# Two of a weight tile's six matmuls made one of 512 columns, its halves added by VectorE

## The reference

```
layer 0:  h = rmsnorm(x); [u | v | z | xbc | dt] = h @ w_in
          x += concat(gmlp(u, v), ssd(z, conv4(xbc), dt)) @ w_out
layer 1:  h = rmsnorm(x); [q | k | v | g] = h @ w_in          # 8 heads
          x += retention(q, k, v, g) @ w_out
each:     h = rmsnorm(x)
          x += (silu(conv3(h @ w_gate)) * (h @ w_up)) @ w_down   # 2816 wide
          x += (p @ w_proj) * sigmoid(rmsnorm(x) @ w_gate_ple)
y = rmsnorm(x)
```

## Time and profile before

| | |
|---|---|
| runs | 1811.79, 1813.09, 1813.15 us (median 1813.09) |
| profiled execution | 1812.7 us, span 1810.9 us |
| granted TensorE clock | 0.996 of full, mean |
| TensorE matmul | 1793.2 us busy, 14029 matmuls |
| VectorE | 930.8 us |
| GpSimd | 834.1 us |
| ScalarE | 635.6 us |
| HBM | 88 GB/s over the span |

### The profile page before, as it was taken

How to read it: one execution, slowest core, us unless ns; L and a number is a source line. 1 busy time by engine, 2 the same in 40 slices (tenths; PEclk the granted TensorE clock), 3 DMA queues, 4 the chain that set the end, 5 groups by cost and what they waited for, 6 DMA issues and landing times.

```text
span 1810.9 us, 34242 instructions
## 1 busy us (share of the span) xinstructions
PE 1793.2 (99%) x14029; PEld 1751.2 (97%) x14029; DVE 930.8 (51%) x1514; ACT 635.6 (35%) x973; POOL 834.1 (46%) x410
## 2 busy tenths in 40 slices
PE   9999999999999999999999999999999999999997
PEld 8999889999999999999999999999899999999997
DVE  6556776666514524546544441444555425515465
ACT  6434564543222222344333331233332213212342
POOL 4323312674545544476533334333365435544663
PEclk9999999999999999999999999999999999999998
DMA  6222232222342232232222222222222222222231
GB/s 236 81 74 72 82 106 72 81 94 94 105 141 82 93 97 91 70 104 83 95 69 76 78 70 91 79 79 69 67 82 93 93 85 89 94 92 85 61 102 50
DMA packets 58389, 161.04 MB, mean 89 GB/s; under 512 B 6817, under 2 KB 19105, under 8 KB 58289
## 3 DMA queue, kind: packets, MB, share of 16 engines
q1 hardware_dynamic: 52224, 151.03, 25.6%
q10 hardware_dynamic: 6064, 8.61, 1.5%
HBM read 153.94 MB, written 5.67 MB: 88 GB/s over the span
## 4 chain that ended last, share of the span: by engine, by line
PE 94%; DVE 3%; ACT 1%; issue 1%; DMA 0%; POOL 0%; ACTq 0%; DVEq 0%; POOLq 0%
PE proj L321 84%; PE Q L1045 7%; PE proj L1045 2%; ACT arena L667 1%; DVE arena L1786 1%; DMA x<-in_x 0%; PE Q L1340 0%; DVE arena L1777 0%; DVE arena L1597 0%; PE Q L1225 0%; DVE arena L1914 0%; PE Q L1271 0%; POOL arena L660 0%; PE Q L1305 0%; DVE rstd L372 0%
## 5 line engine op out<-in xcount | busy, mean ns | idle before, releaser
L417 POOL TENSOR_TENSOR w_lo<-w_raw,w_hi 128x1024 fp32r<-128x1024 f32 (+2 forms) x276 | 663.2, 2404 | 768.0 <-ACT w_hi L343 757.9
L321 PE MATMUL proj<-op_hi,w_hi 128*128 128x256 f32 x4208 | 880.1, 290 | 1.9 <-DVE op_lo L1527 0.8
L321 PE MATMUL proj<-op_hi,w_lo 128*128 128x256 f32 x4208 | 869.3, 288 | 0.0
L321 PE MATMUL proj<-op_lo,w_hi 128*128 128x256 f32 x4208 | 862.2, 286 | 0.0
L321 PEld LDWEIGHTS proj<-op_hi,w_hi 128*128 128x128 f32 x4208 | 671.8, 188 | 17.0 <-issue 12.4
L321 PEld LDWEIGHTS proj<-op_lo,w_hi 128*128 128x128 f32 x4208 | 674.4, 188 | 0.0
L321 PEld LDWEIGHTS proj<-op_hi,w_lo 128*128 128x128 f32 x4208 | 670.4, 188 | 0.0
L343 ACT ACTIVATE w_hi<-w_raw 128x1024 fp32r<-128x1024 f32 (+2 forms) x276 | 284.6, 1031 | 657.8 <-PE proj L321 651.3
L1597 DVE TENSOR_TENSOR arena<-proj,rstd 128x512 f32<-128x512 f32 x141 | 97.5, 691 | 218.4 <-PE proj L321 208.6
L1604 DVE TENSOR_TENSOR x<-proj,x 128x512 f32<-128x512 f32 x72 | 49.7, 690 | 240.3 <-PE proj L321 240.3
L667 ACT ACTIVATE arena<-arena 128x128 f32<-128x128 f32 (+6 forms) x298 | 129.1, 475 | 59.8 <-DVE arena L1600 29.8
(11 more groups left out here) (190 smaller groups left out, 1032.8 us busy)
## 6 DMA issues: line engine op xcount, KB each, us to landing
w_raw<-in_w_gu SPq DMA_DIRECT2D x88, 512.0 KB, 3.4
w_raw<-in_w_down SPq DMA_DIRECT2D x32, 512.0 KB, 3.4
w_raw<-in_w_heads_a SPq DMA_DIRECT2D x30, 512.0 KB, 3.4
w_raw<-in_w_heads_b SPq DMA_DIRECT2D x18, 512.0 KB, 3.4
w_raw<-in_w_gate SPq DMA_DIRECT2D x16, 512.0 KB, 3.4
w_raw<-in_w_xbc SPq DMA_DIRECT2D x12, 512.0 KB, 3.4
w_raw<-in_w_down SPq DMA_DIRECT2D x16, 384.0 KB, 3.1
w_raw<-in_w_v SPq DMA_DIRECT2D x8, 512.0 KB, 8.0
```

Source lines behind the costliest of these rows:

```text
L321: last = nc.tensor.matmul(proj[:, 2 * g.mod(2) + half, 0:size], w[:, lo:lo + P], o[:, at:at + size], start=(k == 0 and j == 0), stop=(k == ...
L417: nc.gpsimd.tensor_tensor(w_lo[:, c:c + width], w_raw[:, c:c + width], w_hi[:, c:c + width], ALU.subtract).then_inc(w_lo_done, 1)
```

## The change

In `slab`, the two matmuls of the high weights over the early tokens, one with the high and one with the low operand, become one of 512 columns. Its moving operand has two runs of 256 columns (the high and low parts, which therefore now lie in one buffer, `op_both`), and its output fills bank `2q`: the first half has high by high, the second high by low. The low weights' product accumulates on the first half. The late tokens keep three matmuls of 288 columns in bank `2q + 1`, so a tile has five matmuls. VectorE adds the halves: in `scaled` and in the up product a `tensor_reduce` writes their sum to a new SBUF buffer `half_sum`, the late half is multiplied straight from PSUM, and the early half is multiplied from `half_sum`; in `add_to_x` the second half is added to x ahead of the rest, with a wait between. The groups in `PLAIN` (v and dt, pp, the last one) keep six matmuls and the old reading.

```diff
--- before.py
+++ after.py
@@ -139,6 +139,12 @@
         return p.g0 + (s - p.s0 + 1) * p.m
 
     DT_GROUP = PH["v"].g0 + KD
+    PLAIN = [*range(DT_GROUP + 1), *(PH[f"pp{layer}"].g0 + m for layer in range(2) for m in range(KD)),
+             PH["gate1"].g0 + KD - 1]
+
+    def summed_before(g):
+
+        return g.c - sum(p < g.c for p in PLAIN)
 
     ctx = ExitStack()
     with ctx:
@@ -154,10 +160,10 @@
 
 
         x = sb("x", KD * T)
-        op_hi, op_lo = [sb("op0_hi", KD * T, R)], [sb("op0_lo", KD * T, R)]
+        op_both = [sb("op0", 2 * KD * T, R)]
         early = nc.sbuf_base
-        op_hi.append(sb("op1_hi", KD * T, R))
-        op_lo.append(sb("op1_lo", KD * T, R))
+        op_both.append(sb("op1", 2 * KD * T, R))
+        op_hi, op_lo = [op[:, 0:KD * T] for op in op_both], [op[:, KD * T:2 * KD * T] for op in op_both]
         ARENA = 15200
         arena = sb("arena", ARENA)
         ssq = sb("ssq", T)
@@ -182,6 +188,7 @@
         a_row = sb("a_row", SH)
         conv_state = sb("conv_state", XBC * 3)
         conv_tail = sb("conv_tail", XBC * 6)
+        half_sum = nc.alloc_sbuf_tensor_at("half_sum", [P, HALF], F, offset=nc.sbuf_base)
         w_dt = sb("w_dt", 8 * SH)
         w_dt_hi = sb("w_dt_hi", 8 * SH, R)
         w_dt_lo = sb("w_dt_lo", 8 * SH, R)
@@ -313,14 +320,23 @@
                     if ready:
                         pe.wait_ge(ready[0], ready[1] + k)
                     lo = slot * SLAB + (k * ph.m + m) * P
-                    passes = ((w_hi, op_hi[ops]), (w_hi, op_lo[ops]), (w_lo, op_hi[ops]))
-                    for j, (w, o) in enumerate(passes):
-                        for half in range(2):
-                            size = HALF if half == 0 else HALF + TS
-                            at = (k0 + k) * T + half * HALF
-                            last = nc.tensor.matmul(proj[:, 2 * g.mod(2) + half, 0:size], w[:, lo:lo + P],
-                                                    o[:, at:at + size], start=(k == 0 and j == 0),
-                                                    stop=(k == ph.kt - 1 and j == 2))
+                    high, low = w_hi[:, lo:lo + P], w_lo[:, lo:lo + P]
+                    first, end = k == 0, k == ph.kt - 1
+                    q = 2 * g.mod(2)
+                    at = (k0 + k) * T
+                    early = slice(at, at + HALF)
+                    late = slice(at + HALF, at + T)
+                    rest = proj[:, q + 1, 0:HALF + TS]
+                    if g.c in PLAIN:
+                        nc.tensor.matmul(proj[:, q, 0:HALF], high, op_hi[ops][:, early], start=first, stop=False)
+                        nc.tensor.matmul(proj[:, q, 0:HALF], high, op_lo[ops][:, early], start=False, stop=False)
+                    else:
+                        nc.tensor.matmul(two(proj[:, q, :]), high, two(op_both[ops][:, :])[:, :, early], start=first,
+                                         stop=False)
+                    nc.tensor.matmul(rest, high, op_hi[ops][:, late], start=first, stop=False)
+                    nc.tensor.matmul(rest, high, op_lo[ops][:, late], start=False, stop=False)
+                    nc.tensor.matmul(proj[:, q, 0:HALF], low, op_hi[ops][:, early], start=False, stop=end)
+                    last = nc.tensor.matmul(rest, low, op_hi[ops][:, late], start=False, stop=end)
                 if ph.kt - 1 in ks:
                     last.then_inc(tile_done, 1)
 
@@ -1590,17 +1606,33 @@
             tt = nc.vector.tensor_tensor
             stt = nc.vector.scalar_tensor_tensor
 
-            def scaled(g, dst, signal=None, rows=P, factor=None, f_at=0):
-
-                by = rstd if factor is None else factor
+            def out_times(g, dst, by, rows=P):
+
                 dve.wait_ge(tile_done, (g + 1).v)
-                a = tt(two(dst(0, TP)), out_prompt(g, rows), two(by[0:rows, f_at:f_at + TP]), mul)
+                if g.c in PLAIN:
+                    return tt(two(dst(0, TP)), out_prompt(g, rows), two(by[0:rows, 0:TP]), mul)
+                q = 2 * g.mod(2)
+                dve.wait_ge(tile_read, g.v)
+                nc.vector.tensor_reduce(half_sum[:, :], proj[:, q, :].rearrange("p (h e) -> p e h", h=2), AX.X, add)\
+                    .then_inc(sem("halves_added"), 1)
+                tt(dst(HALF, HALF), proj[:, q + 1, 0:HALF], by[:, HALF:TP], mul)
+                dve.wait_ge(sem("halves_added"), (g + (summed_before(g) - g.c + 1)).v)
+                return tt(dst(0, HALF), half_sum[:, :], by[:, 0:HALF], mul)
+
+            def scaled(g, dst, signal=None, rows=P):
+
+                by = rstd
+                a = out_times(g, dst, by, rows)
                 if signal:
                     a.then_inc(sem(signal), 1)
-                tt(dst(TP, TS), out_sample(g, rows), by[0:rows, f_at + TP:f_at + T], mul).then_inc(tile_read, 1)
+                tt(dst(TP, TS), out_sample(g, rows), by[0:rows, TP:T], mul).then_inc(tile_read, 1)
 
             def add_to_x(g, n):
                 dve.wait_ge(tile_done, (g + 1).v)
+                if g.c not in PLAIN:
+                    xa = part(x, n, 0, HALF)
+                    tt(xa, proj[:, 2 * g.mod(2), HALF:TP], xa, add).then_inc(sem("halves_added"), 1)
+                    dve.wait_ge(sem("halves_added"), (g + (summed_before(g) - g.c + 1)).v)
                 tt(two(part(x, n, 0, TP)), out_prompt(g), two(part(x, n, 0, TP)), add)
                 tt(part(x, n, TP, TS), out_sample(g), part(x, n, TP, TS), add).then_inc(tile_read, 1)
 
@@ -1772,7 +1804,7 @@
                 at = q * (T + 6)
                 if n >= 2:
                     dve.wait_ge(sem("x_silu"), n - 1)
-                scaled(group("xbc", n), lambda c, w: xpad[:, at + 3 + c + (3 if c else 0):at + 3 + c + (3 if c else 0) + w],
+                scaled(group("xbc", n), lambda c, w: xpad[:, at + 3 + c + (3 if c >= TP else 0):at + 3 + c + (3 if c >= TP else 0) + w],
                        "x_steps")
                 nc.vector.tensor_copy(xpad[:, at + 3 + TP:at + 6 + TP], part(conv_state, n, 0, 3, 3))\
                     .then_inc(sem("x_steps"), 1)
@@ -1898,8 +1930,8 @@
                             at = q * (T + 4)
                             if t.k or t.c >= 2:
                                 dve.wait_ge(sem("f_silu"), (t + -1).v)
-                            scaled(group(gu, n), lambda c, w: gpad[:, at + 2 + c + (2 if c else 0):
-                                                                   at + 2 + c + (2 if c else 0) + w],
+                            scaled(group(gu, n), lambda c, w: gpad[:, at + 2 + c + (2 if c >= TP else 0):
+                                                                   at + 2 + c + (2 if c >= TP else 0) + w],
                                    "f_steps")
                             nc.vector.tensor_copy(gpad[:, at + 2 + TP:at + 4 + TP],
                                                   part(ffn_state, t, 0, 2, 2))\
@@ -1919,9 +1951,8 @@
                             h = hid[:, q * T:(q + 1) * T]
                             g_ = group(gu, n)
                             dve.wait_ge(sem("f_scaled"), (t + 1).v)
-                            dve.wait_ge(tile_done, (g_ + 1).v)
                             gate = fsgr[:, q * T:(q + 1) * T]
-                            tt(two(h[:, 0:TP]), out_prompt(g_), two(gate[:, 0:TP]), mul)
+                            out_times(g_, lambda c, w: h[:, c:c + w], gate)
                             tt(h[:, TP:T], out_sample(g_), gate[:, TP:T], mul).then_inc(tile_read, 1)
                             dve.wait_ge(sem("f_hi"), (t + 1).v)
                             tt(part(op_lo[HID[layer]], n.div(2), 0, T), h, part(op_hi[HID[layer]], n.div(2), 0, T), sub)\
```

## The result

The changed kernel takes **1871.01 us** (median of 5 runs, 1869.32 to 1873.78), the one before 1812.97 beside it on the same chip: a ratio of 1.0323, 95% interval 1.0310 to 1.0336, or 58 us slower. The forecast was 1848 us, so the loss is 23 us larger than forecast and inside the range (1812 to 1874).

A forecast was written before the change was run, and what follows sets the result against it. The prediction took TensorE to bound the kernel before, and VectorE's held loop to bound gate/up afterwards. Gate/up +30.5, matmul saving -5.3 and other phases +10 made +35 us on 1812.7: 1848 us, range 1812 to 1874.

The forecast's parts named there:

- The bound changes hands: Gate/up: VectorE's loop becomes the bound in place of TensorE, by 0.4 us a pair.
- the hold: GpSimd's weight split, about 2.4 us, holds off VectorE's early-half product with two SBUF inputs until it ends.
- the loop: VectorE's time for one gate/up pair: 12.3 us (12.0 to 12.6), against TensorE's 11.92.
- the first rival: Product not held, TensorE stays the bound, matmul excess is per matmul: 1796 us, faster; chance 0.14.
- The pair's steps: Gate/up pair, event by event: up sample 1.85 us later, gate side's first tap at 3.3 us instead of 2.41.
- late rstd: Starts of gu00 and gu10: a 5.4 us late start is no longer caught up; +7.5 us each with its phase.
- The rounds of six pairs: Gate/up phases of six pairs with their down: 4 us longer each.
- The saving: TensorE's dropped matmul saves 4 ns a tile; over 1336 tiles outside gate/up -5.3 us (-0.9 to -15.4).
- The other phases: Outside gate/up, mainly z with outb, xbc and heads: VectorE lateness adds 10 us (3 to 25).
- z, outb, xbc and the heads are bound by VectorE as well: Rival: 25 us or more in these phases and a loop of 12.6 us, about 1880 us; chance 0.12.
- The signs foretold: New profile: gate/up product near 1.7 us, reduce about 0.69, TensorE waits of 3 to 9 us at six down starts.
- The sum: Whole kernel: 30.5 - 5.3 + 10 = +35 us on the profiled run's 1812.7 us.

The follow-up runs named there:

- e10: The changed kernel with GpSimd's weight splits cut to 8 columns after the first four slabs: 1819.90 us, ratio 1.0036 to the kernel before.
- e5: The changed kernel with the late half multiplied first and the sum of the halves written to PSUM instead of half_sum: 1845.55 us against 1813.36.
- e3: The changed kernel's five matmuls alone, with VectorE reading as in the kernel before and no sum of the halves: 1822.44 us against 1814.51.
- e14: The kernel before with its small COPY issued ahead of the group's first product in gate/up and xbc: 1819.98 us, ratio 1.0034.
- e7: The kernel before with its six matmuls in the order of sizes that the change gives them: 1813.40 us, ratio 0.9997.
- e12: The five matmuls with VectorE as before, the low weights' 256 columns moved up behind the 512: 1815.67 us, ratio 1.0010 to the kernel before.
- e11: The five matmuls with VectorE as before, the 512-column matmul reading one contiguous run: 1820.77 us, ratio 1.0042 to the kernel before.
- e6: The changed kernel with its 512-column matmul made two of 256 again, VectorE's added work kept: 1870.24 us against 1813.36 for the kernel before.
- e9: The kernel before with GpSimd's weight splits cut to 8 columns after the first four slabs: 1805.58 us, ratio 0.9955.

## Why the prediction was right in kind and short in size

- **The bound changes hands: right.** With the hold the loop is VectorE's, 12.52 us. Without it (e10, e5) gu01's pairs are 12.04 and 12.07 us apart, TensorE's pace, as the first rival says of a product that isn't held. The rival would still not have come out faster, since nothing is saved.
- **The pair's steps: right.** On the gate side the first tap was put at 3.3 us behind the reduce; it is at 591.03 - 587.78 = 3.25. The low part, which was to get its hold back, is at 0.73. The term that was mis-sized is the loop: two ways gave 12.15 and 12.5 us, and I took 12.3. Gu and down grew by 39.7 us (table), not 30.5, and all of the difference is in the four rounds of eight pairs. In gu01 the first low part ends 13.23 us behind its gate group (12.65 forecast), and the seven that follow are 12.54 us apart. 28 such loops at 0.2 us account for 6 of the 9.2, the half clock at down00 for 1.5. gu00 with down00, after its late rstd, grew by 10.6 (7.5 forecast), gu10 with down10 by 8.6. The rounds of six pairs grew by 3.3 and 4.7 where 4 was forecast, but by luck: their loops are 11.9 us in the mean, not 12.3, and 1.5 of the 4.7 is half clock.
- **The saving: the step that failed.** "so I take a value nearer to the lower end, 4 ns" (a saving of 5.3 us in the rest), and bounds from 0.7 ns up with "the lower end covers it". Measured: 4 ns a tile lost, 8 us by e3. That is the term -5.3 of the sum. The nearest row (last group) gave the price per column rightly: 512 columns cost 233 ns, nearly the two of 256. It could not show what the long matmul does to its neighbours, and a bound on the side of a loss was missing.
- **The other phases: too low.** 10 us were forecast. u, xbc, outb and the heads grew by 16.8 (table), inside the 3 to 25 given and about halfway to the rival "z, outb, xbc and the heads are bound by VectorE as well", which wants 25 or more. xbc was put at 2.5 us (0.7 to 8) and took 6.5, 1.5 of them half clock; u, not in the list, took 2.4; z and outb were put at 3 together and took 0.5 and 2.4; the heads were put at 3.5 and took 5.5. In the heads `rope_cos` is held, as foretold; that it makes all of the 5.5 us no run shows. u's product isn't held (413 ns in the mean of its 8), so its 2.4 us are something else, which no run singles out. In xbc what was overlooked is the hold of the COPY, 1029 ns in the mean and 536 before. In xbc's timeline (VectorE, then GpSimd) it is the COPY at one group, the product at another:

```profile
137.66 0.18 DVE L1628 TENSOR_TENSOR arena<-proj,rstd 128x32 f32<-128x32 f32 x1
137.76 2.25 DVE L1809 COPY arena<-conv_state 128x3 f32<-128x3 f32 x1
...
184.00 1.69 DVE L1620 TENSOR_TENSOR arena<-half_sum,rstd 128x256 f32<-128x256 f32 x1
...
137.57 2.42 POOL L433 TENSOR_TENSOR w_lo<-w_raw,w_hi 128x1024 fp32r<-128x1024 f32 x1 [5.83 <-ACT w_hi L359]
```

- **The signs foretold.** The reduce is at 689 ns (0.69 forecast). The product is at 1449 ns in the up groups and at 1.71 us in the mean of gu's 44 gate groups (1.7 forecast). TensorE does wait at six starts of down, but 2.5 us each and not 3 to 9: it is also held inside the phases, at the up group's sample (L1956, 12 recorded waits), as it can't be more than two groups ahead of VectorE. That this pays off much of the lateness before down is argued, not tested.
- **The sum.** 39.7 + 16.8 us and 0.1 elsewhere, 56.6 from trace to trace; forecast were 30.5 + 10 - 5.3. Of the 21 us that are missing by the traces, 9 are the loop and the starts, 7 the other phases, and 5 the saving that wasn't there. The half clock, of which the sum has no term, is 4.5 us within these parts. All three errors go the same way, and the time stayed inside the range because the range was wide.

On the hold, the Trainium skill, SBUF — State Buffer, "SBUF: two separate sides", names besides an operation with two SBUF inputs also one in a two-port performance mode as a taker of the exclusive lock. The trace agrees in that a COPY with one input, in SBUF, is held as well (158 ns without splits, 1631 in e5); in which mode it ran, no trace shows. The prediction used only the rule's other half.

## What to carry to other kernels

Ask of each new VectorE operation where its inputs lie: beside a GpSimd operation that reads SBUF, 256 columns cost 415 ns from PSUM and up to 2.1 us from SBUF, and making one operation immune passes the hold to the next that isn't. Fewer matmuls with the same columns are no saving until a start-to-start distance shows a fixed part; here six of 272 on average and five of 326 took the same 0.75 us. And where a chain returns to the main engine with no slack, sum the loop event by event: here that sum, 12.5 us, was the right one for the phases of eight pairs. Look also at the granted clock behind each new wait of the main engine.

## What the runs showed of the hardware

- A VectorE COPY of 2 or 3 columns from SBUF to SBUF, 158 ns without splits (e10), took 2.37 us beside a GpSimd split (e14). The prediction spoke only of two SBUF inputs, though its own rows had the first tap, with one tensor as its input, at 2.77 us and at 0.56.
- A 512-column fp32r matmul takes 233 ns to the next start, and in e3 the 288-column steps right behind it and right ahead of it are 4 ns longer each than in e7 (138.5 to 134.1, 132.8 to 128.9). Which part of TensorE causes this stays open; order (e12) reduces it, the operand's layout (e11) doesn't.
- At the end of waits of 2.2 to 3.6 us TensorE's granted clock fell to half for 3.4 us, at three of eight such waits on VectorE in the changed kernel and at six of eight in e6, at a cost of 1.2 to 1.5 us each. Why at these and not at the others, no run shows.
- Without GpSimd's splits the kernel before is 7 us faster (e9), so they cost something there too, by holds or by GpSimd's queue. e14, with the splits kept, moved the COPY and lost 6 us.
